# Writing the weights' remainder over the loaded chunk: four places for chunks, three rounded halves

## The reference

```
first_block:  x += 0.5 * swiglu(rmsnorm(x))                 1024 -> 2816 -> 1024
              x += mixer(rmsnorm(x))      dilated attention in 3 groups, RWKV-7 scan, gates, w_o
              x += 0.5 * swiglu(rmsnorm(x));  final rmsnorm
second_block: twice:  x += 0.5 * swiglu(rmsnorm(x))
                      x += concat(o_a, o_b, o_c) @ w_out     three attentions of 6, 5 and 5 heads
                      x += 0.5 * swiglu(rmsnorm(x))
              final rmsnorm
```

## Time and profile before

| what | us |
|---|---|
| median of three runs | 2114.23 |
| the profiled execution | 2115.32 |
| its span on the core | 2113.5 |
| TensorE (PE) busy | 1926.7 (91%) |
| VectorE (DVE) busy | 1165.1 (55%) |
| ScalarE (ACT) busy | 953.9 (45%) |
| DMA, mean rate over the span | 140 GB/s |
| mean granted TensorE clock | 0.955 of full |

### The profile page before, as it was taken

How to read it: one execution, slowest core, us unless ns; L and a number is a source line. 1 busy time by engine, 2 the same in 40 slices (tenths; PEclk the granted TensorE clock), 3 DMA queues, 4 the chain that set the end, 5 groups by cost and what they waited for, 6 DMA issues and landing times.

```text
span 2113.5 us, 33626 instructions
## 1 busy us (share of the span) xinstructions
PE 1926.7 (91%) x14152; PEld 1713.3 (81%) x14152; DVE 1165.1 (55%) x2284; ACT 953.9 (45%) x1909; POOL 109.1 (5%) x217
## 2 busy tenths in 40 slices
PE   6999988998879899989999678999999998689998
PEld 5999877887767799969997566899899976568998
DVE  4565546654544655645653676556455635865554
ACT  4454554422212545544544454545444535445443
POOL 0000101211111000000001100000000010000000
PEclk9999999998978999999999898999999999889999
DMA  5564424211101455525643212456355523213553
GB/s 193 190 229 171 174 97 145 86 67 49 66 9 66 151 189 206 222 81 190 227 160 122 91 70 100 140 179 242 120 185 207 204 101 120 80 61 132 197 180 120
DMA packets 42518, 296.88 MB, mean 140 GB/s; under 512 B 5136, under 2 KB 5264, under 8 KB 7808
## 3 DMA queue, kind: packets, MB, share of 16 engines
q1 hardware_dynamic: 40608, 288.38, 38.1%
q0 software_dynamic: 1760, 6.36, 0.9%
HBM read 293.67 MB, written 1.05 MB: 139 GB/s over the span
## 4 chain that ended last, share of the span: by engine, by line
PE 79%; DVE 13%; ACT 5%; issue 1%; POOL 1%; DMA 1%; DVEq 0%; SPq 0%; POOLq 0%; ACTq 0%
PE PS L1257 23%; PE PS L1258 22%; PE PS L1259 22%; DVE wlo L2102 1%; ACT GATE L1780 1%; PE PS L1518 1%; PE PS L1537 1%; DVE small L2556 1%; DVE arena L2531 1%; DVE xl L2132 1%; DVE arena L2209 1%; PE PS L1530 1%; PE PS L1285 1%; PE PS L1267 1%; ACT GATE L1786 1%
## 5 line engine op out<-in xcount | busy, mean ns | idle before, releaser
L2102 DVE TENSOR_TENSOR wlo<-raw,whi 128x512 fp32r<-128x512 f32 (+3 forms) x760 | 612.8, 852 | 304.6 <-ACT whi L1773 298.7
L1773 ACT ACTIVATE whi<-raw 128x512 fp32r<-128x512 f32 (+3 forms) x760 | 529.3, 753 | 166.0 <-PE PS L1259 159.7
L1257 PE MATMUL PS<-xh,whi 128*128 128x256 f32 x1944 | 558.3, 287 | 0.0
L1259 PE MATMUL PS<-xh,wlo 128*128 128x256 f32 x1944 | 553.1, 285 | 0.0
L1258 PE MATMUL PS<-xl,whi 128*128 128x256 f32 x1944 | 553.1, 284 | 0.0
L1257 PEld LDWEIGHTS PS<-xh,whi 128*128 128x128 f32 x1944 | 375.7, 193 | 4.1 <-issue 0.7
L1258 PEld LDWEIGHTS PS<-xl,whi 128*128 128x128 f32 x1944 | 376.0, 193 | 2.4
L1259 PEld LDWEIGHTS PS<-xh,wlo 128*128 128x128 f32 x1944 | 375.9, 193 | 0.0
L1257 PE MATMUL PS<-whi,yh 128*128 128x512 f32 (+2 forms) x580 | 228.5, 394 | 8.4 <-DVE wlo L2102 5.4
L1258 PE MATMUL PS<-wlo,yh 128*128 128x512 f32 (+2 forms) x580 | 226.0, 390 | 0.0
L1259 PE MATMUL PS<-whi,yl 128*128 128x512 f32 (+2 forms) x580 | 225.1, 388 | 0.0
(11 more groups left out here) (247 smaller groups left out, 2254.1 us busy)
## 6 DMA issues: line engine op xcount, KB each, us to landing
raw<-wall SPq DMA_DIRECT2D x269, 1024.0 KB, 4.8
arena<-lorap POOLq DMA_DIRECT2D x16, 128.0 KB, 2.7
arena<-ebias POOLq DMA_DIRECT2D x2, 768.0 KB, 5.5
raw<-wall SPq DMA_DIRECT2D x2, 720.0 KB, 4.3
raw<-wall SPq DMA_DIRECT2D x2, 640.0 KB, 3.8
X<-x SPq DMA_DIRECT2D x2, 512.0 KB, 4.1
arena<-rows POOLq DMA_DIRECT2D x1, 1024.0 KB, 9.3
arena<-rows POOLq DMA_DIRECT2D x2, 512.0 KB, 3.7
```

The source lines that it names most:

```text
L1257: e.matmul(o, wa, xa, start=first, stop=False)
L1259: return e.matmul(o, wb, xa, start=False, stop=last)
L1773: e.activation(whi[slot_of(i)][:, c].bitcast(F32R), raw[i % 3][:, c], copy).then_inc(*M.sig("whi", ("split", i, q)))
L2102: e.tensor_tensor(wlo[slot_of(i)][:, c], raw[i % 3][:, c], whi[slot_of(i)][:, c].bitcast(F32), ALU.subtract).then_inc(*M.sig("wlo", *[("ha ...
```

## The change

The remainder `wlo` gets the memory of the loaded chunk: VectorE's subtraction reads `raw` and writes over it. What was three places for loads and two remainders becomes four places `raw0` to `raw3` that are both, and the memory that this leaves goes to a third rounded half; seven buffers of 1 MB before and after. The pairs of leads and of the early down chunk keep their own remainders (now entries 3, 4 and 5). The running chunks take the three halves in turn, and the remainder of chunk i lies in place i % 4. A load into a place now waits, where the chunk there was a running one, for TensorE to have used it (`raw_free`), else for its split. Four loads are issued at the beginning.

```diff
-                out.append(c + (n % 2,))
+                out.append(c + (n % 3,))
...
-        for _ in range(3):
+        for _ in range(4):
             self.feed_dma()
...
     def feed(self):
-        while self.n_split < len(self.chunks) and not any(
-                self.chunks[i][4] < 2 and i not in self.used for i in range(self.n_split)):
+        while self.can_split() and sum(
+                self.chunks[i][4] < 3 and i not in self.used for i in range(self.n_split)) < 1:
             self.feed_split()
...
-        raw = [sb(f"raw{i}", [128, CW]) for i in range(3)]
-        whi = [sb(f"whi{i}", [128, CW], F32R) for i in range(2)]
-        wlo = [sb(f"wlo{i}", [128, CW], F32R) for i in range(2)]
+        raw, wlo = [], []
+        for i in range(4):
+            with nc.sbuf_tensor(f"raw{i}", [128, CW], F32) as t:
+                raw.append(t)
+            wlo.append(sb(f"wlo{i}", [128, CW], F32R))
+        whi = [sb(f"whi{i}", [128, CW], F32R) for i in range(3)]
...
-        def slot_of(i):
-            return P.chunks[i][4]
+        def hi_of(i):
+            return whi[P.chunks[i][4]]
+        def lo_of(i):
+            return wlo_early.get(P.chunks[i][4], wlo[i % 4])
+        def raw_free(i):
+            return ("pe", ("use", i - 4)) if P.chunks[i - 4][4] < 3 else ("wlo", ("split", i - 4))
...
             def load(i):
...
-                if i >= 3:
-                    for t in due(("wlo", ("split", i - 3))):
+                if i >= 4:
+                    for t in due(raw_free(i)):
                         e.wait_ge(*t)
-                e.dma_start(raw[i % 3][:, 0:w], src).then_inc(*M.sig(f"raw{i % 3}", ("chunk", i)))
+                e.dma_start(raw[i % 4][:, 0:w], src).then_inc(*M.sig(f"raw{i % 4}", ("chunk", i)))
...
-                    e.tensor_tensor(wlo[slot_of(i)][:, c], raw[i % 3][:, c], whi[slot_of(i)][:, c].bitcast(F32),
+                    e.tensor_tensor(lo_of(i)[:, c], raw[i % 4][:, c], hi_of(i)[:, c].bitcast(F32),
                                     ALU.subtract).then_inc(
```

More of the change, by code:

```diff
@@ L46, in body @@
                 elif m == 18:
-                    out.append((w, "down", NM // 2 - 1, 2048, 4))
+                    out.append((w, "down", NM // 2 - 1, 2048, 5))
                 out.append((w, "gu", m, 2048))
@@ L83, in plan @@
     work = [s for s in stages if s[0] != "final"]
-    out = [c + (2 + i,) for i, c in enumerate(lead(work[0]))]
+    out = [c + (3 + i,) for i, c in enumerate(lead(work[0]))]
     n = 0
@@ L90, in plan @@
                     i = int(c[4])
-                    out.append(lead(nxt)[i] + (2 + i,))
+                    out.append(lead(nxt)[i] + (3 + i,))
             elif len(c) == 5:
@@ L383, in can_split @@
             return False
-        if self.chunks[i][4] in (2, 3) and self.lead_from is None:
+        if self.chunks[i][4] in (3, 4) and self.lead_from is None:
             return False
@@ L390, in pieces @@
         i = self.n_split
-        after = {2: self.lead_from, 3: self.lead_from, 4: self.last_from}.get(self.chunks[i][4], ())
+        after = {3: self.lead_from, 4: self.lead_from, 5: self.last_from}.get(self.chunks[i][4], ())
         for q in range(n + 1):
@@ L974, in build @@
             M.add(name)
-        for name in ("x0", "x1", "consts", "cols", "raw0", "raw1", "raw2", "masks", "gbias", "bias0", "bias1", "lora0",
+        for name in ("x0", "x1", "consts", "cols", "raw0", "raw1", "raw2", "raw3", "masks", "gbias", "bias0", "bias1", "lora0",
                      "lora1", "rows0", "rows1", "rows2", "gain0", "gain1", "out"):
@@ L1039, in build @@
         whi += [early[0], early[2], early[3]]
-        wlo += [early[1], early[5], early[4]]
+        wlo_early = {3: early[1], 4: early[5], 5: early[4]}
         sp = Space()
@@ L1296, in gu @@
             def gu(s, m, i):
-                hi, lo = whi[slot_of(i)], wlo[slot_of(i)]
+                hi, lo = hi_of(i), lo_of(i)
                 b = bank(("gu", s, m))
@@ L1312, in rows_mm @@
             def rows_mm(name, acc, s, j, kk, tt, nns, i, first, last, sig, a, b, *toks):
-                hi, lo = [t[:, 0:2048].rearrange("p (k n) -> p k n", k=2) for t in (whi[slot_of(i)], wlo[slot_of(i)])]
+                hi, lo = [t[:, 0:2048].rearrange("p (k n) -> p k n", k=2) for t in (hi_of(i), lo_of(i))]
                 for nn in nns:
@@ L1362, in shift_mm @@
             def shift_mm(s, sid, j, k0, i, n, w, end):
-                b, hi, lo = bank(sid), whi[slot_of(i)], wlo[slot_of(i)]
+                b, hi, lo = bank(sid), hi_of(i), lo_of(i)
                 for k in range(k0, k0 + 4):
@@ L1642, in latent_up @@
                     wc = slice(k * w + c0, k * w + c0 + cw)
-                    p = mm3(b[:, 0:cw], yh[:, k0 + k, c], yl[:, k0 + k, c], whi[slot_of(i)][:, wc],
-                            wlo[slot_of(i)][:, wc], k == 0, k == nk - 1)
+                    p = mm3(b[:, 0:cw], yh[:, k0 + k, c], yl[:, k0 + k, c], hi_of(i)[:, wc],
+                            lo_of(i)[:, wc], k == 0, k == nk - 1)
                 p.then_inc(*M.sig("pe", (nm, s, tt, c0), *[("use", i)] * end))
@@ L1769, in split @@
                     c = slice(w * q // n, w * (q + 1) // n)
-                    for t in due((f"raw{i % 3}", ("chunk", i)), P.prev[i] is not None and ("pe", ("use", P.prev[i])),
+                    for t in due((f"raw{i % 4}", ("chunk", i)), P.prev[i] is not None and ("pe", ("use", P.prev[i])),
                                  *(marked(*after) if after else ())):
                         e.wait_ge(*t)
-                    e.activation(whi[slot_of(i)][:, c].bitcast(F32R), raw[i % 3][:, c], copy).then_inc(
+                    e.activation(hi_of(i)[:, c].bitcast(F32R), raw[i % 4][:, c], copy).then_inc(
                         *M.sig("whi", ("split", i, q)))
```

## The result

| | us |
|---|---|
| kernel before, median of 20 runs | 2116.18 (2106.89 to 2122.6) |
| changed kernel, median of 20 runs | 2128.94 (2120.55 to 2135.1) |
| ratio, 95% interval | 1.0055 (1.0041 to 1.0068), so 8.7 to 14.4 us |
| predicted | 2118.5 (2110 to 2124) |

The account below looks back on a forecast made before the run. The prediction took TensorE, busy 91% of the span, as the bound. Zero for the removed wait, subtraction and fourth place plus 4.3 us for late loads made 2119.6, given as 2118.5 us for the median, range 2110 to 2124.

Parts of the forecast that it names:

- The order doesn't run further ahead: In the code's order of steps: one chunk is split per chunk used, so a third half alters no engine's order.
- Rival C: At TensorE's waits for splits: splits do run ahead and remove 18 us of waits, giving 2100.5 us; chance 0.07.
- What removing ScalarE's wait gives: 0: At ScalarE's 159.7 us of waits for a free half: removing them gains 0, bounds 0 and 8 us.
- Rival B: Behind ScalarE's splits: removed waits bring other work forward, up to 8 us, giving 2110.5 us; chance 0.13.
- The subtraction in place: 0: VectorE's 760 subtractions over their input: 0 to 4 ns more each, under 0.1 us on the path.
- The load's wait: the loss: Tails of mix1 and both mix2: loads wait for use(j-4), costing 0.9, 1.7 and 1.7 us.
- the forecast's +0.9: Tail of mix1: wo chunk 2's load waits for use of wo chunk 0, 0.94 us later, all on the path.
- the sum: Over the whole kernel: only the three tails' late loads count, 4.3 us together.
- rival A: Both mix2 tails: the clock falls behind the longer waits, adding 3.2 to 6.4 us, 2121.7 to 2125; chance 0.20.
- The landing: Late loads in the tails: 4.92 us by the trace, used in the sum; the skill's estimate was 4.4 us.
- The range: Whole kernel's time: 2110 to 2124 us for 8 in 10, reaching to most of the slower and faster rivals.

Follow-up runs that it names:

- e5: The changed kernel with feed's bound raised from 1 to 2 split, unused chunks; ratio to before 0.9991, 2114.47 us.
- e7: The changed kernel with three chunks' remainders written into a free rounded half, not over their own place; ratio to before 1.0014, 2118.59 us.
- e6: The changed kernel with three chunks' remainders kept apart and feed's bound raised from 1 to 2; ratio to before 0.9944, 2105.44 us.
- e2: The changed kernel with ScalarE waiting before each running chunk's split as with two halves; ratio to before 1.0042, 2124.24 us.
- e1: The kernel before with only three loads made late, waiting for TensorE's use of the chunk four back; ratio to before 1.0065, 2127.86 us.
- e4: The changed kernel with spare, unread matmuls in the three tails' TensorE waits; ratio to before 1.0027, 2120.58 us.
- e3: The changed kernel with five places for chunks and two rounded halves, loads waiting for use(j-5); ratio to before 1.0014, 2117.99 us.

## Why the prediction was wrong: right in the three late loads, without the clock behind them

- *"The order doesn't run further ahead"*: right. Without the loads, the engines' orders of both kernels are the same step for step (3577 steps, none different), and the 2.47 us start stands. e5 shows the other side: once the bound is raised, the waits fall to 1.9 us. Rival C was priced at 18 us gained; e5's list shows 17.4 us of waits gone, but between e7 and e6 the time falls by 13.2 us.
- *"What removing ScalarE's wait gives: 0"*: right. Waits of 159.7 us became 4.5, those of the evacuation grew by 91.1, and e2, which puts them back, is not distinguishable from the change. Rival B falls.
- *"The subtraction in place: 0"*: the duration is right, 851 ns on average over 760 against 852 before.
- *"The load's wait: the loss"*: right in its three places. For mix2 the working gave a TensorE wait of 2.9 us and +1.7 us each; measured 2.87 and 2.79, and +1.67 and +1.60. In mix1 it gave +0.9: from the last matmul of wo chunk 0 to the first of chunk 2 it was 6.32 us (708.17-701.85) and is 7.08 (713.98-706.90), so +0.76, and +0.88 in e1's stage. The other 0.45 us of the table's 1.21 are lost ahead of the late load, in wo chunk 0's own matmuls, as the windows show. Before, its first matmul is at 695.72 (708.17-12.45):
```profile
694.00:696.00 2.00, 2.00 (x10) 1.90 (x10) 1.61 (x6) 1.32 (x5) 0.00 (x0) 0.50 0.00 0
696.00:698.00 2.00, 2.00 (x9) 1.63 (x8) 1.46 (x4) 0.94 (x3) 0.00 (x0) 0.84 0.00 0
```
and in the changed kernel it is at 700.32 (713.98-13.66):
```profile
699.00:701.00 2.00, 2.00 (x10) 1.90 (x9) 1.81 (x6) 1.61 (x6) 0.00 (x0) 0.50 0.00 0
701.00:703.00 2.00, 2.00 (x8) 1.58 (x7) 1.07 (x4) 1.04 (x4) 0.00 (x0) 0.71 0.00 0
```
A mean of 0.84 is 0.64 us at 0.50, one of 0.71 is 1.16 us: the half clock reaches 0.92 us into the chunk before (696.64) and 1.84 us after (702.16), which is 0.46 us lost. The changed kernel's other two executions have it too. But so has the second execution of the kernel before, and it pays nothing for it: its chunk starts at 698.05 (710.36-12.31), the half clock reaches 1.87 us into it (a mean of 0.77 is 0.92 us at 0.50), and its stretch is 12.31 us, not 12.9. Its window, and a matmul of the first execution:
```profile
699.00:701.00 2.00, 2.00 (x8) 1.57 (x7) 1.07 (x4) 1.04 (x3) 0.00 (x0) 0.77 0.00 0
```
```profile
702.18 0.50 PE L1257 MATMUL PS<-whi,yh 128*128 128x512 f32 x1 [0.33 <-DVE wlo L2102]
```
Before, TensorE had 0.33 us of idle time behind wo chunk 0 that took up the lost time, and the load of wo chunk 2 hung on a split. After, that load hangs on the end of wo chunk 0's use, so time lost to the clock in that chunk comes out again as a later load. The wait before wo chunk 2 follows it: 1.14 us where the half clock reaches 0.9 us into the chunk (e1, e2), 1.46 to 1.57 us where it reaches 1.7 to 1.8 (the changed kernel three times), 1.73 us where it reaches 2.4 (e5). This part of the 1.21 us is the late load's doing too, and the forecast's +0.9, read off one execution, didn't have it.
- *The failed step: the sum ended at 4.3 us and left the clock behind these waits to rival A, with 0.20.* It should have been a term: it measured 1.62+1.60+1.60=4.8 us over the three tails, more than half of their 9.3. The argument "against" in A was that TensorE works densely at 1.00 ahead of these waits as it did ahead of the wait of 2.96 us at 360, which kept its clock. That one case was a poor witness. The same wait of 2.95 us near 360 stands in all twelve traces; behind it the clock stayed at 1.00 in seven and was at 0.50 or just above in five, the first of the changed kernel among them:
```profile
357.43 0.77 PE L1269 MATMUL PS<-whi,yh 128*128 128x512 f32 x1 [2.95 <-DVE yl L2135]
```
```profile
357.40:360.80 3.40, 3.37 (x8) 2.73 (x9) 2.29 (x4) 2.73 (x6) 2.08 (x6) 0.50 0.47 166
```
In the tails it was surer: behind all ten waits of 2.8 to 3.7 us in the mix2 tails (the changed kernel three times, e1 and e2 once) the trace has a stretch of some 3.3 us at 0.50 or just above, and behind none of those of at most 1.19 us. A had only the two mix2 tails; mix1, at 1.46 us, wasn't in it. There the length of the wait doesn't decide it either: behind e5's 1.73 us in the same place the clock stayed at 1.00.
```profile
709.76 0.50 PE L1269 MATMUL PS<-whi,yh 128*128 128x512 f32 x1 [1.73 <-DVE wlo L2114]
```
```profile
709.70:713.10 3.40, 3.17 (x13) 2.32 (x14) 3.40 (x6) 2.20 (x4) 0.00 (x0) 1.00 0.93 369
```
The Trainium skill (TensorE: Matmul & The Clock Gate, HAM oscillation) has the mechanism, a wait for DMA between groups of matmuls after which the next group starts at half speed; the trace agrees, with the 0.50 rows above, though in the changed kernel's tails the half clock sets in only 1.2 to 1.8 us after TensorE has started again (1322.17 and 1323.4 in the first mix2), and e4 shows that matmuls in the wait prevent it.
- *The landing.* The prediction's estimate of 4.4 us by the Trainium skill (DMA: Bandwidth & Descriptors, Anatomy of one DMA) comes from a fit for DMAs that GpSimd issues; these loads are issued by SP. The late load took 4.88 us (1313.02 to 1317.90), near the 4.92 that the sum used.
- *The range.* 4.3+4.8 is 9.1 us, and upon 2114.2 that gives 2123.3, just under the top of 2124. The median of 20 runs of the kernel before is itself 2.0 us above that of the three shown, and some 3 us more are not located in the tails. The top should have taken in A and both of these.

**Open.** From the medians the change costs 12.8 us, the tails 9.3. The remaining 3.5 us lie within the interval's width, and e3, e4 and e7 each stand 1 to 3 us further above the kernel before than their tails say (e3 and e7 at 1.0014, with intervals that begin 0.0001 and 0.0002 above 1). But e1, which has none of the new buffers, is 12.5 us above with tails 7.9 us longer, and so leaves 4.6 us over too. TensorE's idle time, span less busy time, says what kind of time it is: 186.8 and 185.7 us in the two executions of the kernel before, 191.1, 191.8 and 189.6 in the three of the changed kernel. The waits grew by 3 to 6 us, around the forecast's 4.3, and all else is matmuls at the lower clock. The mean granted clock is 0.95175 over the 20 executions of the changed kernel and 0.95471 over 56 of the kernel before. From these numbers, as an estimate, the changed kernel spends some 12.6 us more at 0.50 (0.00296 of 2126 us, twice); the three stretches of the tails are 10.2 us of it. What is left, some 2 us at 0.50 or 1 us of time, is less than two executions of one kernel differ by: the attention stages move by 4 us between them. Whether the late loads also move the clock's falls there, or the new buffers cost a little, these runs don't tell.

## What to carry to other kernels

When a buffer gets a second life, work out for each load who frees it now and how much slack it had: here three loads of some 270, in the tails where splits follow one another, made the loss, and three buffers kept apart took most of it away. More buffers bring nothing unless the written order runs further ahead, so change the bound with them (0.9944 with it, 1.0014 without; the bound without the third half wasn't run). Price a TensorE wait that grows to some 3 us twice, as idle time and as half-clock work behind it, and don't take one execution in which the clock held as proof that it will.

## What the runs showed of the hardware

- Waits of 2.8 to 3.7 us behind work at 1.00 were followed by half clock in ten cases of ten in the mix2 tails; a wait of 2.95 us near 360 was in five traces of twelve. In mix1's tail waits of 1.46 to 1.57 us were, in three executions, one of 1.73 us was not (e5), and behind waits of 1.14 us the stretch was as before (e2) or 0.4 us longer, at 1.00 (e1). In a mix2 tail 1.6 us more of idle time cost 3.2 us.
- Matmuls without use, run during the same wait, kept the clock at 1.00 and gave back 4.8 us in three places.
